# A two-layer hybrid trunk on one core: attention's TensorE order, the adaLN gate rows and the expert choice rearranged

## What is computed

```python
mod = silu(c) @ w_ada[l] + b_ada[l]             # 6 vectors of 1024
sh1, sc1, g1, sh2, sc2, g2 = split(mod, 6)
h = rms_norm(x) * (1 + sc1) + sh1
q, k, v, qi, ki, wi, cu = split(h @ w_in[l])    # 3144 columns
# q, k: norm per head and rope; qi, ki: the indexer's, 8 heads of 64
score = sum_h wi[h] * relu(qi[h] . ki)          # causal; the best 64 keys per token
attn = softmax over the chosen keys, 8 heads
conv = silu(layer_norm(depthwise_conv31(a * sigmoid(g))))
x = x + g1 * (concat(rms(attn), rms(conv)) @ w_out[l])
h2 = rms_norm(x) * (1 + sc2) + sh2
# PEER: per head (8): 16 best of 128 keys twice, 16 best of their sums -> 16 experts of 16384
g = softmax(top16);  act = gelu(h2 . u[e])
x = x + g2 * sum_{head, k} g * act * v[e]
```

## Time and profile before

| | |
|---|---|
| median of 3 runs | 1929.71 us (1923.74 to 1929.81) |
| profiled execution | 1930.05 us, span 1927.8 us |
| PE busy | 1098.2 us (57%) |
| DVE busy | 1015.4 us (53%) |
| POOL busy | 992.1 us (51%) |
| ACT busy | 297.4 us (15%) |
| DMA | 696.06 MB, 361 GB/s mean over the span |
| weights (queue of SP) | 156.58 MB |
| rows of experts and other loads of POOL | 538.24 MB |

### The profile page before, as it was taken

One profiled execution on the slowest core, in us unless ns is written; L12 is line 12 of the kernel. 1 busy time (PEld: TensorE's weight loads), 2 busy tenths in 40 slices (PEclk: granted clock), 3 DMA queues, 4 the chain that ended last, 5 costly groups with the idle time before them and its releaser, 6 DMA issues.

```text
span 1927.8 us, 19711 instructions
## 1 busy us (share of the span) xinstructions
PE 1098.2 (57%) x7062; PEld 631.2 (33%) x7062; DVE 1015.4 (53%) x2647; ACT 297.4 (15%) x842; POOL 992.1 (51%) x1072
## 2 busy tenths in 40 slices
PE   5997887757167555858066555948167550003554
PEld 4764655444034114544044114634044110000110
DVE  1142287679736406687826307687836309994000
ACT  2342112342000002451010002442010000000000
POOL 2000007335555776344654776334655777776774
PEclk9997877876579787987588887977678675556888
DMA  8646599968999999998999999988999999999998
GB/s 300 210 158 241 207 325 398 400 249 329 404 407 398 404 410 407 391 347 313 406 406 402 383 409 406 395 294 297 405 406 369 378 409 410 410 410 409 409 409 324
DMA packets 230913, 696.06 MB, mean 361 GB/s; under 512 B 23958, under 2 KB 23974, under 8 KB 230818
## 3 DMA queue, kind: packets, MB, share of 16 engines
q0 software_dynamic: 148080, 538.24, 71.5%
q1 hardware_dynamic: 82738, 156.58, 22.5%
HBM read 693.70 MB, written 1.05 MB: 360 GB/s over the span
## 4 chain that ended last, share of the span: by engine, by line
DMA 34%; PE 19%; POOL 13%; DVE 12%; issue 6%; ACT 3%; POOLq 0%; ACTq 0%; DVEq 0%
DMA rows<-in_peer_v,v_at 16%; DMA rows<-in_peer_u,u_at 11%; POOL rows L489 8%; DMA wring<-in_w_in 7%; PE ps L623 6%; DVE rows L1016 6%; PE ps L582 5%; POOL rows L481 5%; PE ps L571 3%; PE ps L540 2%; ACT diag_eq L843 1%; PE ps L604 1%; PE ps L520 1%; PE ps L698 1%; ACT hT L809 1%
## 5 line engine op out<-in xcount | busy, mean ns | idle before, releaser
L481 POOL DMA_INDIRECT rows<-in_peer_u,u_at x512 | 483.0, 943 | 661.0 <-DVE dots L1016 284.5
L1016 DVE CUSTOM_DVE_ANT_0 rows<-rows,ps 128x1024 f32<-128x1024 f32 x512 | 605.8, 1219 | 216.4 <-DMA rows<-in_peer_u,u_at 205.4
L489 POOL DMA_INDIRECT rows<-in_peer_v,v_at x512 | 497.7, 972 | 253.3 <-issue 131.9
L623 PE MATMUL ps<-rows,spread_c 128*32 128x512 f32 x2048 | 343.2, 804 | 272.4 <-DMA rows<-in_peer_v,v_at 272.4
L623 PEld LDWEIGHTS ps<-rows,spread_c 128*32 128x32 f32 x2048 | 74.4, 131 | 513.1 <-issue 511.5
L571 PE MATMUL ps<-wring,hT 128*128 128x512 f32 x384 | 191.3, 654 | 43.7 <-DMA wring<-in_w_in 32.5
L582 PE MATMUL ps<-hT,wring 128*128 128x128 f32 x1536 | 186.3, 285 | 15.3 <-ACTq L813 13.2
L582 PEld LDWEIGHTS ps<-hT,wring 128*128 128x128 f32 x1536 | 183.4, 201 | 24.0 <-ACTq L813 18.8
L520 PE MATMUL ps<-ident,coef 128*128 128x128 f32 x4 | 1.9, 476 | 325.2 <-DVE coef L1261 325.2
L843 ACT ACTIVATE diag_eq<-ident,cwT 128x128 f32<-128x128 f32 x496 | 148.4, 387 | 35.2 <-PE ps L604 33.3
L571 PEld LDWEIGHTS ps<-wring,hT 128*128 128x128 f32 x384 | 78.3, 211 | 143.9 <-issue 90.0
(11 more groups left out here) (192 smaller groups left out, 910.8 us busy)
## 6 DMA issues: line engine op xcount, KB each, us to landing
wring<-in_w_ada SPq DMA_DIRECT2D x48, 1024.0 KB, 8.7
wring<-in_w_in SPq DMA_DIRECT2D x48, 1024.0 KB, 14.6
wring<-in_peer_wq SPq DMA_DIRECT2D x32, 1024.0 KB, 16.4
wring<-in_w_out SPq DMA_DIRECT2D x16, 1024.0 KB, 10.7
rows<-in_peer_u,u_at POOLq DMA_INDIRECT x512, 11.9
rows<-in_peer_v,v_at POOLq DMA_INDIRECT x512, 9.1
wring<-in_w_in SPq DMA_DIRECT2D x4, 288.0 KB, 23.1
out_x<-xs SPq DMA_DIRECT2D x2, 512.0 KB, 4.6
```

The source lines that it names most:

```text
L481: pool.indirect_dma_start(row(n), None, u_rows, bass.IndirectOffsetOnAxis(ap=u_at[:, p % 2, k:k + 1], axis=0)).then_inc(row_landed[n % SLO ...
L489: pool.indirect_dma_start(row(n), None, v_rows, bass.IndirectOffsetOnAxis(ap=v_at[:, p % 2, tok:tok + 1], axis=0)).then_inc(row_landed[n % ...
L623: ins = pe.matmul(ps[32 * g:32 * g + 32, YB + q, :], spread_c[:, g, a, :], row(n)[:, q * 512:q * 512 + 512], start=a == 0, stop=a == 31)
L1016: dve.tensor_tensor_reduce(out=row(n), in0=row(n), in1=h2_shown, scale=1.0, scalar=0.0, op0=ALU.mult, op1=ALU.add, accum_out=dots[:, k:k + ...
```

## The change

Five things change together.

1. **Order of first(p).** qi, ki, q, k are projected first, then the index operands and products; cg and ca follow, then the turns of q and k, the first logits, v, and only then the convolution's first pair. The other seven pairs stand between the softmax sets (`CONV_BETWEEN`). ScalarE's diagonals move with them, and the SiLU comes behind the last set. VectorE's GLU product and its convolution norm move behind the selection and behind the logits, and the numbers of dot products between the steps change.
2. **Gate rows.** All 24 adaLN blocks are computed narrow. For the gate blocks the turn is a product with a broadcast column of the identity (4 matmuls of 128 columns), which spreads the row.
3. **Places of the adaLN blocks.** Layer 0's blocks 6 to 9 stand behind the last values of part 0 ("mix"), four blocks of layer 1 between the expert queries; the gate blocks (0,10), (0,11) and layer 1's blocks 8 and 9 in the tail of part 0. Part 1 has none.
4. **Expert numbers per pair of heads.** `decode(p, blk)` follows each `choose(p, blk)`, over 128x512 elements, and POOL waits for every 32 numbers. In part 0 VectorE does dot products between the pairs, up to 10, 22 and 34. TensorE shows h2 in PSUM ahead of the expert queries.
5. **First loads.** The DMA of x's first block comes behind the first four halves of weights.

The diff, cut to its core; lines that begin with # and the remarks behind `more_dots` are added here to say where they stand.

```diff
+FIRST_DOTS = (0, 10, 22, 34)
+CONV_BETWEEN = [((1, 2, 3), (4, 5), (6,), (7,)),
+                ((1,), (2,), (3,), (4,), (5,), (6,), (7,), ())]
 ADA = {
     (0, "pre"): [(0, 0), (0, 1), (0, 2), (0, 3)],
-    (0, "dots"): [(0, 4), (0, 5)],
-    (0, "qk"): [(0, 6), (0, 7)],
-    (0, "S"): [(0, 8), (0, 9)],
-    (0, "qp"): [(0, 10), (0, 11)],
-    (0, "tail"): [(1, 0), (1, 1), (1, 2), (1, 3), (1, 6), (1, 7)],
-    (1, "S"): [(1, 8), (1, 9)],
+    (0, "S"): [(0, 4), (0, 5)],
+    (0, "mix"): [(0, 6), (0, 7), (0, 8), (0, 9)],
+    (0, "qp1"): [(1, 0), (1, 1)],
+    (0, "qp2"): [(1, 2), (1, 3)],
+    (0, "tail"): [(1, 6), (1, 7), (1, 8), (1, 9), (0, 10), (0, 11)],
     (2, "S"): [(1, 4), (1, 5)],
     (3, "S"): [(1, 10), (1, 11)],
 }
...
             for p in range(PARTS):
-                pool.wait_ge(sel_ready, p + 1)
                 for k in range(P):
+                    if k % 32 == 0:
+                        pool.wait_ge(sel_ready, 4 * p + k // 32 + 1)
...
+                        if b_ in ROW_BLOCKS:
+                            b, o = open_job("adaT", l, b_)
+                            for q in range(4):
+                                ins = pe.matmul(o[:, q * P:(q + 1) * P], ident[:, 32 * q:32 * q + 1].to_broadcast([P, P]),
+                                                st, start=True, stop=True)
...
 # TensorE, first(p)
-                proj_turned(("cg", p), ("cg", p), hT)
-                proj_turned(("ca", p), ("ca", p), hT)
                 proj(("qi", p), hT)
-                conv(p, 0)
...
-                conv(p, 1)
-                for i, name in enumerate(("q", "k", "v")):
-                    proj((name, p), hT)
-                    conv(p, 2 + i)
+                proj(("q", p), hT)
+                proj(("k", p), hT)
...
-                conv(p, 6)
-                ada(p, "dots")
+                proj_turned(("cg", p), ("cg", p), hT)
+                proj_turned(("ca", p), ("ca", p), hT)
...
+                pe.wait_ge(qkT_ready, 2 * (p + 1))
                 logits(ns[0])
+                proj(("v", p), hT)
+                conv(p, 0)
...
                 for i, n in enumerate(ns):
                     if n != ns[-1]:
                         logits(n + 1)
+                    for pair in taps[2 * i]:
+                        conv(p, pair)
                     if i:
                         values(n - 1)
                     if i == len(ns) - 1:
                         ada(p, "S")
                     pe.wait_ge(exp_ready, 6 * l + n + 1)
                     turn4(("PT", l, n), [ex[:, n % 2, j * P:(j + 1) * P] for j in range(4)])
+                    for pair in taps[2 * i + 1]:
+                        conv(p, pair)
                 values(ns[-1])
+                ada(p, "mix")
...
 # ScalarE, first(p), the end
                     evac(("PT", l, n), pt[:, n % 2, :], ptT_ready)
+                    for pair in taps[2 * i + 1] + (taps[2 * i + 2] if i + 1 < len(ns) else ()):
+                        make_diags(p, pair)
+                ada(p, "mix")
+                act.wait_ge(silu_in, p + 1)
+                act.activation(hb[:, AW:D], hb[:, AW:D], ACT.Silu).then_inc(silu_done, 1)
...
 # VectorE, first(p): dot products between the steps
-                more_dots(14)            # norm of x -> GLU product
-                more_dots(10)            # -> index key
+                more_dots(10)            # norm of x -> index key
-                more_dots(14)            # -> q, k
+                more_dots(10)
-                more_dots(8)             # -> index scores, 2, selection
+                more_dots(6)
-                more_dots(8)             # -> convolution norm, 3, logits 0 and 1, SiLU, (3, logits) ..., 8
+                more_dots(6)             # -> GLU product
                 logits(ns[0])
+                more_dots(4)
                 logits(ns[1])
+                for n in ns[2:]:
+                    more_dots(4)
+                    logits(n)
+                more_dots(10)            # -> convolution norm, 4, SiLU, attention norm
...
 # VectorE, second(p)
-                choose(p)
-                decode(p)
+                for blk in range(4):
+                    choose(p, blk)
+                    decode(p, blk)
+                    if p == 0:
+                        dots_to(0, FIRST_DOTS[blk])
+                finish_choice(p)
```

More of the change, by code:

```diff
@@ L116, in plan @@
             job("dot", l, n)
-        ada(p, "dots")
+        for name in ("cg", "ca"):
+            block(name, p)
+            job(name, p)
         job("qT", p)
         job("kT", p)
-        ada(p, "qk")
+        ns = CHUNKS[t]
+        job("S", l, ns[0])
+        block("v", p)
+        job("v", p)
         if t == 0:
@@ L419, in _ @@
             for i, (name, h) in enumerate(uses):
+                if i == WSLOTS:
+                    sp.dma_start(xs[:, 0, :], x[0, 0:P, :]).then_inc(x_landed[0], 16)
                 slot = i % WSLOTS
-                if name == ("cg", 2) and not done_small:
+                if name == ("qi", 2) and not done_small:
                     sp.wait_ge(qk_ready, 2)
@@ L550, in ada @@
                     pick = ident[0:L * 12, r:r + 1]
[L551 to L560 removed]
+                    plus_one = b_ // 2 in (1, 4)
+                    for q in range(4):
+                        oq = o[32 * q:32 * q + 32, 0:P]
+                        ins = pe.matmul(oq, pick.to_broadcast([L * 12, 32]), brow[:, q * P:(q + 1) * P],
+                                        start=False, stop=not plus_one)
+                        if plus_one:
+                            ins = pe.matmul(oq, ones[0:1, 0:32], ones[0:1, :], start=False, stop=True)
                     ins.then_inc(full[b], 1)
@@ L702, in first @@
                 ns = CHUNKS[t]
+                pe.wait_ge(qkT_ready, 2 * (p + 1))
                 logits(ns[0])
+                proj(("v", p), hT)
+                conv(p, 0)
+                if t == 0:
+                    raw = half(("sk", p), 0, 16)
+                    for n in range(4):
+                        turn4(("skT", p, n), [raw[:, 4 * n + i, :] for i in range(4)])
+                pe.wait_ge(proj_ready, 5 * (p + 1))
+                taps = CONV_BETWEEN[t]
                 for i, n in enumerate(ns):
@@ L741, in second @@
                 pe.wait_ge(skT_ready, 4 * (l + 1))
+                if p:
+                    pe.wait_ge(u_used, p * P)
+                for k in range(KT):
+                    ins = pe.transpose(ps[:, HB + k // 4, (k % 4) * P:(k % 4 + 1) * P], hT[:, k, :], ident[:, :])
+                ins.then_inc(h2_in_psum, 1)
                 def subkeys(b_):
@@ L1281, in _ @@
             take_y(PARTS - 1)
-STAGE_PLACES = [(p, where) for p in range(PARTS) for where in ("pre", "dots", "qk", "S", "qp", "tail")]
+STAGE_PLACES = [(p, where) for p in range(PARTS) for where in ("pre", "S", "mix", "qp1", "qp2", "qp3", "tail")]
 _INS = ["x", "c", "positions", "w_ada", "b_ada", "w_in", "q_norm_g", "k_norm_g", "idx_k_ln_g",
```

230 lines of the change are left out of this document (96 added, 134 removed).

## The result

The changed kernel takes 1982.59 us (1977.0 to 1986.94, 4 runs), the kernel before beside it 1928.99 (1923.74 to 1929.81, 4 runs): a ratio of 1.0282, 95% interval 1.025 to 1.0314. It is slower by 2.8%; I had forecast 0.9% faster, and the time lies outside my range. From experiment e6 on, everything took some per cent longer, the kernel before 2053 to 2056 us (the slower condition, shown at the end), so each kernel is compared with the kernel before, or with its sibling, of its own set of runs.

What follows compares the result with a forecast made beforehand. Bound by the start of the first rows, then VectorE's chain in three u phases, then DMA; -19 + 10 - 8 = -17 on 1930.05 gave 1913, 1912.5 at the median; own range 1897 to 1924, wider 1882 to 1940.

Steps and rivals of the forecast that it cites:

- a wait of 34 us for the convolution: Part 2's u phase: convolution full at 128 after h, VectorE there at 94, so one wait of 34 us.
- The step on the u phases: U phases, counted from h by VectorE's work and waits: part 1 19 us less, part 2 10 more, part 3 8 less.
- 54: Part 2: the convolution is full 54 us after the GLU product (at 74), with two softmax sets and two adaLN blocks.
- The wait for the last values: Parts 2 and 3: VectorE's wait of 12.0 and 11.4 us behind two wide gate blocks goes with narrow gates.
- Part 1: H at 341.4, attention norm 140 us later, 42 for the remaining products and rows: u phase ends at 523.5, 19 us less.
- rival A: Rows crowd out weights: at 10 us a half, third scores at 299 instead of 277; slower, 1957 in full; chance 0.17.
- the 8.5 from which I let A decide: Weight halves beside the rows: from about 8.5 us a half, crowding out by rows decides the outcome.
- My 7.4: Weights beside expert rows: a half of 1 MB takes 7.4 us, by the distance of qi's two halves.
- the wait of 1 us for the third scores: Part 0, expert choice: VectorE waits some 5 us for the second scores and 1 us for the third.
- The rule that DMA engines take turns between queues: Weights beside rows: even shares give 5.2 us a half, u phases 7 us shorter each, 21 in all: 1892.
- The gates: Narrow gate rows: nothing counted in part 0, where DMA sets the pace; at least 0, at most 23 us, within the waits.
- my sum of -17: Whole kernel: the u phases of parts 1, 2 and 3 change by -19, +10 and -8 us, -17 on 1930.05.

Runs made afterwards that it cites:

- e6: The changed kernel with ScalarE making only one diagonal per batch from pair 1 on, the others stale: 2016.62 us, ratio 0.9799 to the kernel before.
- f4: The changed kernel with v projected directly behind ca, before the logits, in the slower condition: 2049.22 us, ratio 0.9996 to the kernel before.
- e3: The changed kernel with VectorE's GLU product put ahead of the index scores and the selection: 1952.34 us, ratio 1.0126 to the kernel before.
- e1: The changed kernel with the old order of first(p) and layer 0's adaLN blocks in their old places: 1895.33 us, ratio 0.9842 to the kernel before.
- g3: g4's kernel with POOL waiting for all four pairs and no dot products between them in part 0: 2039.29 us, ratio 0.9931 to the kernel before.
- g4: e1's kernel run again, in the slower condition, as the base for g3: 2030.53 us, ratio 0.9892 to the kernel before.
- e2: The kernel before with only the gate rows narrow, all blocks in their old places: 1908.74 us, ratio 0.9904 to the kernel before.
- e4: The changed kernel with the four adaLN blocks between the expert queries moved into the tail: 1990.18 us, ratio 1.0338 to the kernel before.
- f1: The changed kernel unedited, run again in the slower condition as a base: 2070.67 us, ratio 1.009 to the kernel before.
- f3: The kernel before with one diagonal made per batch from pair 1 on, the others stale, slower condition: 2030.91 us, ratio 0.9899 to the kernel before.
- h1: The kernel before with stale diagonals but ScalarE's full number of instructions, unused ones written to a spare tile: 2056.49 us, ratio 1.0015 to the kernel before.

## Why the prediction was wrong

**What held.** In part 0 the convolution was to be full at 155 and was at 155.5: projections first, then seven pairs at ScalarE's 4.6 us. From the GLU product that is 68 us said (87 to 155) and 70.0 measured. The attention norm was to come at 180.6 and came at 186.0, the first row at 244.6 and 250.35, both 5 to 6 late. In part 2 I had forecast a wait of 34 us for the convolution; it is 38.8. Waits in that phase: 66.3 us instead of my 46.5. The v phases kept their length (198.0 and 196.5 against 199.9 and 200.5).

**The step on the u phases failed, by the sizes of its waits.** The way of counting was sound for parts 2 and 3: in part 2 VectorE's waits grew from 42.9 us (the sum of that phase's waits before, rows included) to 72.2, by 29.3, and the phase by 31.8; in part 3 from 42.8 to 52.6, by 9.8, and the phase by 11.6. Its waits in part 3 after:

```profile
DVE mixed_use L1128 <- PE ps L680: 24.9, 3, 9.1
DVE hb L1107 <- ACTq L806: 10.3, 1, 10.3
DVE rows L1020 <- DMA rows<-in_peer_u,u_at: 6.1, 8, 0.8
DVE bn L1150 <- PEq L615: 5.7, 1, 5.7
DVE bn L1092 <- ACTq L806: 4.0, 1, 4.0
DVE gy L984 <- ACT hb L920: 1.4, 1, 1.4
```

| waits, us | part 2 said | measured | part 3 said | measured |
|---|---|---|---|---|
| index key | 2.5 | 3.9 | 2.5 | 4.0 |
| q and k | 9 | 12.0 | 9 | 10.3 |
| logits | 0 | 11.6 | 7 + 6 | 24.9 |
| convolution | 34 | 38.8 | 2 | 5.7 |
| SiLU and the rest | 1 | 0 | 3 | 1.4 |
| sum | 46.5 | 66.3 | 29 (29.5 by its terms) | 46.3 |

Two terms carry it, the logits (11.6 and 11.9 more) and the convolution (4.8 and 3.7 more), and both hang on the same thing. In the u phases I let v follow the first logits freely, and there was no term for a PSUM bank. TensorE waits 10.6 us there in part 2 with the second logits queued behind v and, behind them, the taps. From the GLU product the convolution took 70.8 us in part 2 and not 54: 10.1 to v's end (840.06 to 849.3) and then 60.6 for eight pairs, copies, exponentials and two adaLN blocks, where ScalarE and TensorE wait for each other in turn and three pairs run at a lower clock.

The 54 did not fit my own part 0. There I had put v (7 us) and the first pair (4) one behind the other after the GLU product and come to 68, and 70.0 was measured; part 2 has the same two sets and eight pairs. With 68 in part 2 the convolution would have been full at 142 after h and not 128, and the wait 48: the mistake was there to be found before any run. f4 and e3 open the chain and take back 21.5 us (in the slower condition) and 30 us, f4 by parts 1 and 3 and what lies behind them.

**Where I looked for a gain, little came in parts 2 and 3.** The wait for the last values, 12.0 and 11.4, did go with the narrow gates: 1.9 and 1.7 in e1. But in e1's part 2 VectorE's waits for rows rose from 5.9 to 11.2, the index key's from 12.3 to 14.1 and ca's from 4.5 to 5.8. Of the 10.1 us that went, 8.4 came back; the phase is 1.5 us shorter there and 2.2 in part 3. The new order then traded a wait for the index key of 14.1 us (e1) for one of 3.9, and bought logits and a convolution that are waited for 50.4 us (part 2).

**Part 1.** I had h at 341.4; it came at 363.8. 5.4 us are the late attention norm, 2.6 the second scores (a wait of 7.6, not 5), 16.5 the third (17.5, not 1), less 2 elsewhere. That is rival A's place and nearly its number: it put the third scores at 299, they came at 301.5. But it did not need its slow halves. TensorE's timeline shows when the halves are used:

```profile
256.80 1.96 PE L553 MATMUL ps<-wring,cact 128*32 128x128 f32 x64
267.55 1.94 PE L553 MATMUL ps<-wring,cact 128*32 128x128 f32 x32 [8.21 <-DMA wring<-in_w_ada]
275.59 1.94 PE L553 MATMUL ps<-wring,cact 128*32 128x128 f32 x32 [6.10 <-DMA wring<-in_w_ada]
...
290.48 9.46 PE L588 MATMUL ps<-hT,wring 128*128 128x128 f32 x64 [11.00 <-issue]
299.78 2.10 PE L759 MATMUL ps<-skT,mixed_use 128*128 128x128 f32 x16
```

8.0 us between two halves of a block, and 14.9 until the query block behind them starts, which needs both of its halves: 7.4 to 8.0 a half, below the 8.5 from which I let A decide. My 7.4 was right. The step that failed is the wait of 1 us for the third scores: four halves land beside the rows ahead of them, the first used at 267.55 and the last at 290.48, and the forecast didn't lay them end to end at its own 7.4. Only A counted halves there, and at 10 us each. The rule that DMA engines take turns between queues (the Trainium skill, page "DMA: Bandwidth & Descriptors", section "Queues, rings and completion order") would by even shares have given 5.2 us a half, an estimate; these 7.4 to 8.0 us disagree with it as the 7.4 of the trace before did. The time for it, 1892, would have been wrong too.

Part 1's u phase was to be 182 us and was 199.7: 153.4 and not 140 up to the attention norm, 46.3 and not 42 behind it. I had priced the whole part at -19, and by the marks up to the first coefficients it is +20.4; of the rows' head start alone a gain of 8.8 us is shown (g3, g4).

**The gates** I put at nothing in part 0 and within the sum of waits elsewhere; alone they are worth 17.4 us (e2), and part 0's attention norm comes 9.5 us sooner. There I had said that DMA sets the pace of these blocks, which those 9.5 us contradict.

**The comparison that I didn't make.** Each step was set against the kernel before, and none asked what the other parts would give without the order. e1 says: 1895.33. The order costs 4.5% of that (1.0282/0.9842), and my sum of -17 stood for two effects of opposite sign, -33.4 and +85.5 by the spans.

**What stays open.** Of the 85.5 us that the order costs (e1), 24 are in part 0, where I had forecast a delay (7 against the kernel before; against e1 it is 24), and 62 behind it. The GLU product's place takes back 30. In the slower condition, where the order costs 2.0% (1.009/0.9892), or some 40 us, v's place takes back 21.5, and ScalarE's diagonals are worth 36 more than in the kernel before. Whether fewer diagonals and an open chain together would return all, I did not try.

Where the order gets cheaper in the slower condition shows in the waits. In g4, e1's kernel, VectorE's waits in the u phase of part 2 are 61.4 us instead of e1's 40.4, and the phase is 248.1 instead of 227.2. In the change they are 67.4 instead of 72.2, and the phase 258.5 instead of 260.5. The old order's wait for ca has grown from 5.8 us:

```profile
DVE hc L1092 <- PE ps L586: 21.0, 1, 21.0
```

In that phase TensorE stands still seven times, 12.3 us in all, inside the projections of cg and ca, which the old order has first: between two matmuls, with nothing in the profile that they wait for. So the price of the order, 4.5% or 2.0%, hangs on a condition of the chip as well.

## What to carry to other kernels

The sum of one engine's waits was the right measure of the u phases of parts 2 and 3 here, to 2.5 us; what has to be listed with more care is everything that can make a moved job wait. When a job is moved, follow its output bank as well as its operands: with a ring of four, the job waits for the reader of the job four places earlier. When two stages have the same chain, compare the two lengths that were forecast for it. When a change has parts, price each against the others' result, and build the one that leaves out the part with the longest new wait.

## What the runs showed of the hardware

Two things differ between the runs up to e4 and those from e6 on. The first is the rate of the DMA engines. Both lines below are the same kernel, the change, in 40 slices of its span; the first is the run of 1981.70 us, the second that of 2077.74 (f1). In the eight slices before the last the first moves 403 to 410 GB/s and the second 343 to 402. In other slices the second reaches 404 to 410 as well.

```profile
GB/s 281 272 79 200 231 367 388 397 389 205 276 405 397 406 410 405 350 263 201 406 410 401 404 409 408 356 279 279 394 410 400 403 409 410 410 410 409 406 409 322
```
```profile
GB/s 284 246 100 228 225 396 395 344 365 160 346 404 396 379 362 392 387 134 350 410 374 383 370 349 395 368 184 335 408 376 314 373 367 402 369 376 343 361 366 300
```

The second is that TensorE stands still in the middle of its work in the later runs. "issue" is idle time that ends with nothing that the profile shows. The projections of L586 in one kernel, e1 (first line) and g4 (second), over the whole span (us, times, longest):

```profile
PE ps L586 <- issue: 16.4, 3, 10.9
```
```profile
PE ps L586 <- issue: 58.1, 47, 5.3
```

e1's three stand ahead of a block of weights. Of g4's 58.1 us, 44 lie between two matmuls of one block, of which the second waits for no semaphore; in f1, with the new order, such stops of the same projections (L588) are 17 us, and in e1 and the change there are none. The kernel before takes 6.6% longer in that condition (1926 and 2053 us), the change 4.4% (1982.59 and 2070.67), so that its loss falls from 2.8 to 0.9%. What sets the condition, and whether its two signs are one thing, is open.

And ScalarE, busy 15% of the span, is worth 1% of the time in the kernel before when three quarters of its diagonals are left out (f3, h1, in the slower condition), though VectorE waits for no convolution there: what shrinks are its waits for ScalarE's copies and for ca.
